# Two transformer blocks on one core: latent attention by pairs of heads, queries scaled beforehand, and the scaling of a pair's probabilities placed behind the next pair's scores

## What is computed

```python
# first block
mod = silu(c) @ w_ada + b_ada                      # six rows of 1024: shift, scale, gate, twice
h = rms(x) * (1 + sc1) + sh1
x = x + g1 * hybrid_mixer(h)                       # SSD branch, dilated attention, pooling, gated and summed
h = rms(x) * (1 + sc2) + sh2
x = x + g2 * (relu(h @ w_ff1) ** 2 @ w_ff2)
# second block, 256 context tokens beside the 512; layers 0 and 3 window attention, 1 latent attention, 2 mLSTM
for i in range(4):
    h = rmsnorm(x, g_pre) * (1 + sc) + sh
    x = x + gate * rmsnorm(mixer[i](h), g_post)
# layers 0 and 3: 16 heads of 64, window of +-128 keys and all context keys, a sink logit per head
logits = q @ k * 64 ** -0.5
m = max(max(logits), sink); e = exp(logits - m); p = e / (sum(e) + exp(sink - m))
# layer 1: 8 heads, 128 columns without and 64 with rotary position (one rotary key for all heads)
logits = (q_nope @ k_nope + q_rope @ k_rope) * 192 ** -0.5; p = softmax(logits)
```

## Time and profile before

| | |
|---|---|
| median of 3 runs | 3556.99 us (3556.87 to 3562.08) |
| the profiled execution's own time | 3554.6 us |
| its span in the trace | 3552.8 us |
| mean granted TensorE clock | 0.92 of full |
| busy: PE, PEld, DVE, ACT, POOL | 84%, 67%, 53%, 33%, 21% |
| chain that ended last: PE, DVE, ACT, issue, DMA | 65%, 24%, 6%, 3%, 1% |

### The profile page before, as it was taken

The page is one execution under the profiler, slowest core; times in us unless marked ns, Lnnn a source line. Parts: engine busy times, 40 slices in busy tenths (PEclk is TensorE's granted clock), DMA queues, the critical chain, the costliest instruction groups (busy, mean ns, idle before and its releaser), DMA issues.

```text
span 3552.8 us, 40086 instructions
## 1 busy us (share of the span) xinstructions
PE 2989.8 (84%) x16196; PEld 2369.3 (67%) x16196; DVE 1891.2 (53%) x3705; ACT 1163.6 (33%) x1990; POOL 741.7 (21%) x160
## 2 busy tenths in 40 slices
PE   4956977787999999999778797999799877579876
PEld 2834855566777788779566575558599766458565
DVE  5984255553733999810776502444820477560574
ACT  2323233333213222232464433332522200242462
POOL 2401412221433444322001121002122100013101
PEclk8988988898999999999999997999999887799998
DMA  6600421221233555321001111001113200312101
GB/s 250 237 12 24 166 86 57 107 107 36 83 124 129 190 193 186 139 83 60 13 1 60 72 60 36 1 1 72 72 60 107 84 1 1 119 71 83 36 2 60
DMA packets 49031, 291.12 MB, mean 82 GB/s; under 512 B 4304, under 2 KB 5584, under 8 KB 19280
## 3 DMA queue, kind: packets, MB, share of 16 engines
q1 hardware_dynamic: 22464, 163.59, 12.8%
q10 hardware_dynamic: 26384, 124.98, 9.2%
HBM read 267.58 MB, written 20.97 MB: 81 GB/s over the span
## 4 chain that ended last, share of the span: by engine, by line
PE 65%; DVE 24%; ACT 6%; issue 3%; DMA 1%; ACTq 0%; DVEq 0%; PEldq 0%
PE psum L411 16%; PE psum L412 16%; PE psum L413 16%; PE psum L1306 5%; DVE ada_temp L713 3%; PE psum L1469 2%; PE psum L1325 2%; DVE pair_prob L1518 2%; PE psum L861 2%; PE psum L1315 1%; PE psum L2486 1%; PE psum L1477 1%; DVE conv L954 1%; DVE a_lo L870 1%; DVE h L884 1%
## 5 line engine op out<-in xcount | busy, mean ns | idle before, releaser
L398 POOL TENSOR_TENSOR w_lo<-raw,w_hi 128x2048 fp32r<-128x2048 f32 x156 | 741.5, 4753 | 2769.1 <-ACT w_hi L406 2769.1
L411 PE MATMUL psum<-a_hi,w_hi 128*128 128x512 f32 (+3 forms) x1880 | 704.3, 375 | 98.3 <-DVE a_lo L870 62.4
L412 PE MATMUL psum<-a_lo,w_hi 128*128 128x512 f32 (+3 forms) x1880 | 698.6, 372 | 0.0
L413 PE MATMUL psum<-a_hi,w_lo 128*128 128x512 f32 (+3 forms) x1880 | 697.6, 371 | 0.0
L713 DVE SCALAR_TENSOR_TENSOR ada_temp<-ada_ring,ada_rows 128x1024 f32<-128x1024 f32 x240 | 439.9, 1888 | 92.5 <-DMA ada_ring<-ada 77.7
L411 PEld LDWEIGHTS psum<-a_hi,w_hi 128*128 128x128 f32 (+1 forms) x1880 | 356.8, 190 | 182.2 <-issue 70.3
L413 PEld LDWEIGHTS psum<-a_hi,w_lo 128*128 128x128 f32 (+1 forms) x1880 | 356.8, 190 | 62.9 <-issue 2.3
L412 PEld LDWEIGHTS psum<-a_lo,w_hi 128*128 128x128 f32 (+1 forms) x1880 | 357.4, 190 | 58.4 <-issue 0.6
L406 ACT ACTIVATE w_hi<-raw 128x2048 fp32r<-128x2048 f32 x156 | 298.0, 1911 | 260.0 <-DMA raw<-stream 110.3
L412 PE MATMUL psum<-w_lo,a_hi 128*128 128x256 f32 x800 | 226.4, 283 | 0.0
L413 PE MATMUL psum<-w_hi,a_lo 128*128 128x256 f32 x800 | 226.4, 283 | 0.0
(11 more groups left out here) (388 smaller groups left out, 5091.8 us busy)
## 6 DMA issues: line engine op xcount, KB each, us to landing
raw<-stream SPq DMA_DIRECT2D x156, 1024.0 KB, 4.8
ada_ring<-ada ACTq DMA_DIRECT2D x72, 1024.0 KB, 5.3
xres<-x_in ACTq DMA_DIRECT2D x4, 3072.0 KB, 10.1
x_in<-xres ACTq DMA_DIRECT2D x3, 3072.0 KB, 11.4
gates<-gate_part ACTq DMA_DIRECT2D x8, 768.0 KB, 4.5
c_z<-gates ACTq DMA_DIRECT2D x1, 3072.0 KB, 16.9
c_og<-gates ACTq DMA_DIRECT2D x1, 2304.0 KB, 9.9
x<-xT ACTq DMA_DIRECT2D x1, 2048.0 KB, 16.8
```

Source lines behind the costliest of these rows:

```text
L398: pool.tensor_tensor(k.w_lo[:, r], k.raw[:, r], k.w_hi[:, r].bitcast(F32), ALU.subtract) \
L411: pe.matmul(out, lhs[0], rhs[0], start=start, stop=False)
L412: pe.matmul(out, lhs[0], rhs[1], start=False, stop=False)
L413: return pe.matmul(out, lhs[1], rhs[0], start=False, stop=stop)
```

## The change

The change has five parts.
- **Start.** x is loaded ahead of the condition's row and the modulation slots, SP's first weight loads wait for x, and the silu of the row comes behind the squares.
- **Modulation.** The eight slots of the `xbc` projection move to the gated projection of `ssd_out` (`gated`, 16 tiles), with rows of their own.
- **Queries** leave their projection multiplied by minus the scale; the operation of mask and extremum takes a minimum against the sink, and the exponential has the scale -1 and that minimum as its bias. The negation (L1521) goes, and the sink is copied only where the head changes.
- **Scaling.** Masked scores go to a buffer of their own (`row`), exponentials to `prob`. DVE makes the reciprocal of both units of pair p-1 and scales them behind the masks of pair p, and behind a `finish` if there is one.
- **Latent attention** uses `pair_attention`: 4 pairs of heads by 6 blocks. The two units' 128-row scores come first, then the 64-row ones of both in turn. PE then makes values of 2p-4, transposes of 2p-2, values of 2p-3, transposes of 2p-1.

```diff
@@ weight_stream @@
     @block.sync
     def _(sp):
+        sp.wait_ge(k.sem_named("residual_loaded").sem, 16)
         for s in range(RING_SLOTS):
             load_slot(k, sp, s)
@@ dense @@
-    assert not (turns > 1 and ada)
-    share = ada.share(n_t) if ada else None
+    share = ada.share(total) if ada else None
@@ setup @@
-        first_ada.load_rows(act)
         act.dma_start(x1[:], k.io["xT"].rearrange("(c p) t -> p c t", p=P)) \
             .then_inc(k.sem_named("residual_loaded").sem, 16)
+        first_ada.load_rows(act)
         for s in FIRST_ADA:
             first_ada.load(act, s)
@@ ssd_branch @@
-    ada = k.ada.group(16, B0 + 40960, k.ARENA + 32768 + 8192, k.ARENA + 32768, 3)
+    ada = k.ada.group(8, B0 + 40960, k.ARENA + 32768 + 8192, k.ARENA + 32768, 3)
...
-          dve_tile=conv_tile, ada=ada.of(8),
+          dve_tile=conv_tile,
@@ ssd_out (gated passes ada on to dense) @@
-    gated(k, block, a, y, [f"{x}{c}" for c in range(4) for x in ("g_ssd", "ssd_out")], acc, B0)
+    gated(k, block, a, y, [f"{x}{c}" for c in range(4) for x in ("g_ssd", "ssd_out")], acc, B0,
+          ada=k.ada.group(8, B0 + 49152, B0 + 86016, B0 + 81920, 3, new_rows=True).of(8))
@@ first_block: the silu of the condition goes behind the squares @@
-        first_ada.silu_rows(act)
         act.wait_ge(loaded.sem, loaded.at(16))
...
+    def first_row(act):
+        first_ada.silu_rows(act)
...
-             before_chunk=lambda dve, c: modulation_start(k, first_ada, dve, c), after_root=first_weights)
+             before_chunk=lambda dve, c: modulation_start(k, first_ada, dve, c), after_root=first_weights, then=first_row)
@@ pair_attention, tensor @@
+            for u in (2 * p, 2 * p + 1):
+                for col, cols, q, keys in units[u].get("whole", ()):
+                    pe.matmul(score(u)[:, col:col + cols], q, keys, start=True, stop=False)
+            first = "whole" not in units[2 * p]
             for one, other in zip(units[2 * p]["qk"], units[2 * p + 1]["qk"]):
                 for u, (col, cols, q, keys) in ((2 * p, one), (2 * p + 1, other)):
-                    last = pe.matmul(score(u)[:, col:col + cols], q, keys, start=True, stop=True)
+                    last = pe.matmul(score(u)[:, col:col + cols], q, keys, start=first, stop=True)
...
+            if halves:
+                if 1 <= p <= n:
+                    turn(2 * p - 2)
+                if p >= 2:
+                    values(p - 2, (2 * p - 4, 2 * p - 3))
+                if 1 <= p <= n:
+                    turn(2 * p - 1)
+            else:
+                if 2 <= p:
+                    values(p - 2, (2 * p - 4,))
+                if 1 <= p <= n:
+                    turn(2 * p - 2)
+                if 2 <= p:
+                    values(p - 2, (2 * p - 3,))
+                if 1 <= p <= n:
+                    turn(2 * p - 1)
@@ pair_attention, vector @@
-            dve.tensor_copy(prob[:, u % 4, w:w + 1], un["sink"])
+            if sinks and (u < 4 or units[u - 4]["head"] != un["head"]):
+                dve.tensor_copy(row[:, u % 4, 0:1], un["sink"])
             dve.wait_ge(scores_done.sem, scores_done.at(u // 2 + 1))
...
-            dve.wait_ge(masked.sem, masked.at(u + 1))
-            dve.tensor_scalar(st[:, 1:2], st[:, 0:1], -scale, un["neg_sink"], ALU.mult, ALU.min) \
-                .then_inc(negated.sem, 1)
...
+        def scale_probs(p):
+            at = 2 * p % 4
+            dve.wait_ge(exp_done.sem, exp_done.at(2 * p + 2))
+            ch(dve, dve.reciprocal(stat[:, 2, at:at + 2], stat[:, 1, at:at + 2]))
+            for u in (2 * p, 2 * p + 1):
+                w = len(units[u]["pv"]) * P
+                dve.tensor_scalar(prob[:, u % 4, 1:1 + w], prob[:, u % 4, 1:1 + w], stat[:, 2, u % 4:u % 4 + 1],
+                                  None, ALU.mult).then_inc(scaled.sem, 1)
...
-            if p < n:
-                scale_prob(2 * p)
-                scale_prob(2 * p + 1)
+            if 1 <= p <= n:
+                scale_probs(p - 1)
@@ pair_attention, scalar @@
-            act.wait_ge(negated.sem, negated.at(u + 1))
-            act.activation(prob[:, u % 4, 0:w + 1], prob[:, u % 4, 0:w + 1], ACT.Exp, bias=st[:, 1:2],
-                           scale=scale, accum_out=st[:, 2:3]).then_inc(exp_done.sem, 1)
+            act.wait_ge(masked.sem, masked.at(u + 1))
+            if u >= 4:
+                act.wait_ge(turned.sem, turned.at(u - 3))
+            act.activation(prob[:, u % 4, c0:1 + w], row[:, u % 4, c0:1 + w], ACT.Exp,
+                           bias=stat[:, 0, u % 4:u % 4 + 1], scale=-1.0, accum_out=stat[:, 1, u % 4:u % 4 + 1]).then_inc(exp_done.sem, 1)
@@ gqa_layer @@
-    dense(k, block, [f"A{l}q"], feature_major(a, KC, parts), turn_slots=2, act_tile=into(q, ACT.Copy, parts),
+    dense(k, block, [f"A{l}q"], feature_major(a, KC, parts), turn_slots=2, act_tile=into(q, ACT.Copy, parts, -A_SCALE),
...
-    pair_attention(k, block, pairs, temp, A_SCALE)
+    pair_attention(k, block, pairs, temp, 640, True, True)
@@ mla_layer @@
-    attention(k, block, units, R0 + 73728, 768)
+    def unit_of(h, b):
...
+        return dict(whole=[(512 * n, k1 - k0, q[:, h, t], kn[:, h, k0:k1]) for n, (k0, k1) in enumerate(keys)],
+                    qk=[(512 * n, k1 - k0, qr[r0:r0 + 64, h // 2, t], kpe[r0:r0 + 64, k0:k1])
+                        for n, (k0, k1) in enumerate(keys)],
+                    mask=0, pv=[v[:, kb, h * P:(h + 1) * P] for kb in blocks])
...
+        if b == 5:
+            pair["finish"] = finish_both(c)
...
+    pair_attention(k, block, [pair_of(c, b) for c in range(4) for b in range(6)], R0 + 73728, 768, False, False)
```

More of the change, by code:

```diff
@@ L1204, in ssd_branch, with gated @@
     k.end_stage(block)
-def gated(k, block, a, b, sections, acc, temp, m=None, rhs_ready=None):
+def gated(k, block, a, b, sections, acc, temp, m=None, rhs_ready=None, ada=None):
     first = m is None
@@ L1236, in gated @@
     dense(k, block, sections, lambda s, hi, lo: feature_major(b if s else a, KC, [(0, S)])(s, hi, lo),
[L1237 removed]
+          turn_slots=2, act_tile=take, dve_tile=project, ada=ada, barrier=False)
 def ssd_out(k, block, a, acc):
@@ L1438, in attention, with pair_attention @@
     k.end_stage(block)
-def pair_attention(k, block, pairs, temp, scale):
-    scores_done, masked, negated, exp_done, scaled, turned, copied, out_done, out_taken = (
-        k.sem_named(f"pair_{x}") for x in ("scores_done", "masked", "negated", "exp_done", "scaled", "turned",
-                                           "copied", "out_done", "out_taken"))
+def pair_attention(k, block, pairs, temp, wide, sinks, halves):
+    scores_done, masked, exp_done, scaled, turned, copied, out_done, out_taken = (
+        k.sem_named(f"pair_{x}") for x in ("scores_done", "masked", "exp_done", "scaled", "turned", "copied",
+                                           "out_done", "out_taken"))
     n = len(pairs)
-    wide = 640
-    prob = k.at("pair_prob", temp, [P, 4, wide + 8])
-    prob_t = k.at("pair_prob_t", temp + 16 * wide + 128, [P, 4, wide])
-    mask = k.at("pair_mask", temp + 32 * wide + 128, [P, wide])
-    stat = k.at("pair_stat", temp + 36 * wide + 128, [P, 4, 8])
+    row = k.at("pair_row", temp, [P, 4, wide + 8])
+    prob = k.at("pair_prob", temp + 16 * wide + 128, [P, 4, wide + 8])
+    prob_t = k.at("pair_prob_t", temp + 32 * wide + 256, [P, 2 if wide > 640 else 4, wide])
+    n_t = 2 if wide > 640 else 4
+    mask = k.at("pair_mask", temp + 32 * wide + 256 + 4 * n_t * wide, [P, wide])
+    stat = k.at("pair_stat", temp + 36 * wide + 256 + 4 * n_t * wide, [P, 3, 4])
     units = [u for pair in pairs for u in pair["units"]]
@@ L1476, in turn, with values @@
             for j in range(len(units[u]["pv"])):
-                last = pe.transpose(turn_bank[:, j * P:(j + 1) * P], prob[:, u % 4, j * P:(j + 1) * P],
+                last = pe.transpose(turn_bank[:, j * P:(j + 1) * P], prob[:, u % 4, 1 + j * P:1 + (j + 1) * P],
                                     k.cst("ident"))
             last.then_inc(turned.sem, 1)
-        def values(p):
-            pe.wait_ge(copied.sem, copied.at(2 * p + 2))
-            if p >= 2:
+        def values(p, us):
+            pe.wait_ge(copied.sem, copied.at(us[-1] + 1))
+            if p >= 2 and us[0] == 2 * p:
                 pe.wait_ge(out_taken.sem, out_taken.at(p - 1))
@@ L1486, in values @@
             for j in range(n_blocks):
-                for u in (2 * p, 2 * p + 1):
-                    r0 = 64 * (u % 2)
-                    last = pe.matmul(k.psum[r0:r0 + 64, 6 + p % 2, 0:P], units[u]["pv"][j],
-                                     prob_t[:, u % 4, j * P:(j + 1) * P], start=j == 0, stop=j == n_blocks - 1)
-            last.then_inc(out_done.sem, 1)
+                for u in us:
+                    last = pe.matmul(value_bank(u), units[u]["pv"][j], prob_t[:, u % n_t, j * P:(j + 1) * P],
+                                     start=j == 0, stop=j == n_blocks - 1)
```

(30 more changed lines are left out.)

73 lines of the change are left out of this document (38 added, 35 removed).

## The result

| | before | after |
|---|---|---|
| median of 4 runs | 3559.53 us (3556.87 to 3565.44) | 3787.39 us (3781.17 to 3790.16) |
| ratio | | 1.0637, 95% interval 1.0619 to 1.0654 |
| the profiled execution | 3554.6 us | 3784.77 us |
| its span | 3552.8 us | 3782.9 us |
| mean granted clock | 0.92 | 0.89 |

What follows compares the result with a forecast made beforehand. Four engines' steps in a loop bound the window layers, PE latent attention. Window pairs +117, context pairs +15, latent attention +22, first block -5 and -11 gave +138; the clock +108 on 3554.6 gave 3800 us, range 3690 to 3880.

Steps and rivals of the forecast that it cites:

- The gap in the window layers: Window attention: PE idles behind each pair's scores until DVE's masks and scaling end, 2.5 us for 5 key blocks; +117 us, context pairs +15.
- the finish: Window attention: DVE's finish, between masks and scaling, enters the loop: 1.79 us in one latent pair of four, 0.45 on average.
- The clock in the window layers: Window layers: gaps pull PE to 1.2 GHz two fifths of the time, as in the mLSTM layer; +59 us, context pairs +8.
- Latent attention: Latent layer: per two heads 13.4 us of gaps against 7.9 saved by pairing scores, +22 us in all; low clock +41 more.
- The first block: Kernel start and xbc projection: earlier first scaling of x, -5 us, and fewer DVE products in xbc, -11 us.
- xbc: xbc projection: DVE loses 16 products and ends some 5 us behind PE's last tile instead of 16; -11 us, bounds -6 and -13.
- the start: Kernel start: x lands 8 to 9 us earlier, DVE's first scaling at 28 instead of 33.09; -5 us, bounds -9 and +3.
- The moved products: Gated projection: 16 products of 1.98 us, 32 us, covered by PE's 86 us; costed at nothing, 11 us if that failed.
- The clock stays at 2.4 GHz: Rival: full clock holds since each gap is followed by 3.6 us or more of unbroken work; 3693 us, chance 0.18.
- 64-row scores don't overlap: Rival, latent attention: the 64-row scores of 512 columns do not overlap, 31 us more, 3831 us; chance 0.07.
- Low clock throughout: Rival: the low clock holds nearly throughout, as nothing lifts a loop that once runs slowly; some 4050 us, chance 0.05.

Runs made afterwards that it cites:

- experiment 3: Changed kernel with unused 128x128 matmuls filling PE's gaps in the window layers, PE still waiting for the scaling: 3694.77 us.
- experiment 5: Changed kernel with the scaling of pair p-1 ahead of the masks of pair p, and latent attention unit by unit as before: 3522.85 us.
- experiment 6: Changed kernel with the eight modulation slots multiplied in the xbc projection again, not in the gated projection: 3792.85 us.
- experiment 2: Changed kernel with the finish of a chunk moved behind the scaling, instead of between masks and scaling: 3702.89 us.

## Why the prediction was right

3800 was forecast and 3787.39 measured, inside the range, and slower as said. By its steps:

- **The gap in the window layers** stood as worked out: 2.5 us forecast behind the scores of 5 key blocks, 2.58 of idle time measured (2.20 for 4 blocks, where the forecast came to 2.0); the finish 1.79 forecast, 1.79 measured (1743.45 to 1745.24). Layers 0 and 3 at full clock took 76.2 and 58.9 us more (experiment 3); the terms gave 58.5 + 15 = 73.5, and 58.5.
- **The clock in the window layers** was right in kind and too small: 37.5 and 29.5 us forecast, 54.0 and 36.2 measured. Taking the mLSTM layer's two fifths of the time at 1.2 GHz was right for layer 3, where 0.81 is 38%, and low for layer 0, where 0.76 is 48%. What that choice left out is that layer 0 also has context pairs, with idle 1.5 or 2.7 us for every 2.0 to 3.1 us of matmuls: the clock is 0.70 in them and 0.79 in the latent pairs. In layer 3 the price was 6.7 us too small although the share was right: my sum spread the low clock evenly over gaps and work, but PE's busy time rose from 120.7 to 157.7 us, so most of it fell on the work.
- **Latent attention** was the mis-sized term: 22 + 41 = 63 forecast, 20.5 measured. Its parts on DVE held: gaps of 12.2 us per two heads for 13.4, with the joint finish 4.9 for 4.9. Three sizes failed. The pairing takes 10.1 us off PE's work per two heads and not 7.9 (experiment 5), so two heads should take 39.9 + 12.2 = 52.1 us at full clock and not 55.5. I took the mLSTM layer's clock for it, 0.8; it is 0.88, 24% of the time, and with the 57.5 measured the clock costs 5.4 us per two heads and not 10.3. And I set 50.0 us per two heads as the pace before, from one head at full clock; the layer of before opens with 22 us at 1.2 GHz, shown above, and with its ends it averages 214.6 / 4 = 53.7, against 235.1 / 4 = 58.8 after.
- **The first block**: -16 forecast, -15.2 measured. Of it xbc is -12.8 (forecast -11) and the start -2.5 (forecast -5): x landed at 12.0 us for 18.9 before, 6.9 earlier and not 8 to 9; DVE's first scaling came at 29.7 and not at 28, and its second operation ran beside POOL. The moved products were hidden, as said, to within the 1.5 us of experiment 6.
- Measured less forecast, the clock in the window layers gives +23 and latent attention -43. They cancel in part, so that the total came within 13 us is partly luck.
- **The rivals.** "The clock stays at 2.4 GHz" gave 3693, and experiment 3, which keeps it up in the window layers, gave 3694.77 (partly by chance, as latent attention still ran at 0.89); but the changed kernel lets it fall. "64-row scores don't overlap" is refuted by 1.49 us for eight. "Low clock throughout" did not come.
- By the Trainium skill, "TensorE: Matmul & The Clock Gate", section "Why this matters for your kernels", the throughput of TensorE drops in mid-kernel behind idle gaps longer than those of experiment 2; the gaps of 4.1 and 6.2 us here are long enough for it, the plain ones of 2.2 and 2.6 are not. The runs disagree on the plain ones: in experiment 2, where no gap of the window layers is longer than 2.67 us, the clock is 0.82 and 0.85.

Open is why layer 0 has a clock of 0.75 to 0.78 from run to run with one and the same loop (most of the spread lies in its context pairs, 0.63 to 0.72), and what in the 22 us at the head of latent attention holds the clock down while PE is busy.

## What to carry to other kernels

When a step of the last item is put behind a step that waits for the next item's result, look at which engine needs the first one next: VectorE sat idle 5.7 us ahead of the masks, where the scaling could have run, and two lines of its list were worth 296 us. Price a new gap twice, bare and with the clock that it lets fall: here 135 and 90 us in the window layers. And when one wait is removed, list again what ends last: the copy on ScalarE was worth nothing until the scaling was in its place, and 35 us afterwards.
